# A fourth gate slab as seven block products in groups 2 to 8 of both feed-forward networks

## What is computed

```
x = x + 0.5 * _swiglu(_rmsnorm(x, ffn_norm), w_gu, w_down)

def _swiglu(h, w_gu, w_down):
    gate, up = jnp.split(h @ w_gu, 2, axis=-1)
    return (jax.nn.silu(gate) * up) @ w_down
```

## Time and profile before

| | us |
|---|---|
| median of 3 runs | 3013.56 |
| lowest, highest | 3011.37, 3015.36 |
| profiled execution, its own time | 3013.77 |
| its span in the trace | 3012.0 |
| TensorE busy | 2990.2 (99%) |
| VectorE busy | 2138.6 (71%) |
| GpSimd busy | 1531.6 (51%) |
| ScalarE busy | 1502.0 (50%) |

### The profile page before, as it was taken

The page is one execution under the profiler, slowest core; times in us unless marked ns, Lnnn a source line. Parts: engine busy times, 40 slices in busy tenths (PEclk is TensorE's granted clock), DMA queues, the critical chain, the costliest instruction groups (busy, mean ns, idle before and its releaser), DMA issues.

```text
span 3012.0 us, 48048 instructions
## 1 busy us (share of the span) xinstructions
PE 2990.2 (99%) x19120; PEld 2671.4 (89%) x19120; DVE 2138.6 (71%) x3446; ACT 1502.0 (50%) x1999; POOL 1531.6 (51%) x749
## 2 busy tenths in 40 slices
PE   8999999999999999999999999999999999999998
PEld 7888888888999999998888888888899998999997
DVE  4889886764324447787688887777579866789764
ACT  6555544444667455544555554444544454534454
POOL 5887764445565555585578876444550004710013
PEclk9999999999999999999999999999999999999999
DMA  6888887885776555566688888788576546666455
GB/s 217 288 278 271 278 280 247 305 288 181 229 176 176 158 165 148 151 171 201 200 284 282 266 281 287 242 306 277 173 216 194 162 147 216 181 190 182 154 182 181
DMA packets 491671, 663.43 MB, mean 220 GB/s; under 512 B 70440, under 2 KB 278040, under 8 KB 490936
## 3 DMA queue, kind: packets, MB, share of 16 engines
q1 hardware_dynamic: 485960, 655.85, 68.2%
q0 software_dynamic: 4448, 2.94, 0.4%
q10 hardware_dynamic: 1040, 1.58, 0.2%
HBM read 656.06 MB, written 2.11 MB: 219 GB/s over the span
## 4 chain that ended last, share of the span: by engine, by line
PE 95%; DVE 3%; ACT 1%; DMA 0%; issue 0%; POOL 0%; DVEq 0%; ACTq 0%
PE ps L1142 33%; PE ps L1006 20%; PE ps L1147 17%; PE ps L1012 10%; PE ps L1023 3%; PE ps L1175 2%; PE ps L1028 1%; PE ps L1171 1%; PE ps L990 1%; PE ps L1667 1%; DVE narrow_split_slabs L2261 1%; PE ps L1181 1%; PE ps L1443 1%; PE ps L1424 1%; PE ps L1178 1%; DVE h_split L2218 1%
## 5 line engine op out<-in xcount | busy, mean ns | idle before, releaser
L925 POOL TENSOR_TENSOR split_slabs<-stage,split_slabs 128x1024 fp32r<-128x1024 f32 x366 | 892.3, 2447 | 1005.4 <-ACT split_slabs L1723 999.4
L1723 ACT ACTIVATE split_slabs<-stage 128x1024 fp32r<-128x1024 f32 x544 | 573.4, 1059 | 558.3 <-PE ps L1147 435.8
L1723 ACT ACTIVATE narrow_split_slabs<-stage 128x1024 fp32r<-128x1024 f32 (+1 forms) x437 | 457.3, 1050 | 589.1 <-PE ps L1012 442.5
L1142 PE MATMUL ps<-split_slabs,h_split 128*128 128x512 f32 x2904 | 719.6, 390 | 0.8 <-ACT split_slabs L1723 0.8
L1142 PEld LDWEIGHTS ps<-split_slabs,h_split 128*128 128x128 f32 x2904 | 541.7, 188 | 111.4 <-ACT split_slabs L1723 1.2
L1006 PE MATMUL ps<-h_split,narrow_split_slabs 128*128 128x256 f32 x4928 | 620.6, 279 | 3.1 <-issue 1.9
L925 POOL TENSOR_TENSOR narrow_split_slabs<-stage,narrow_split_slabs 128x1024 fp32r<-128x1024 f32 (+1 forms) x182 | 441.2, 2434 | 315.8 <-ACT narrow_split_slabs L1723 315.5
L1006 PEld LDWEIGHTS ps<-h_split,narrow_split_slabs 128*128 128x128 f32 x4928 | 586.7, 188 | 13.0 <-issue 7.7
L2261 DVE TENSOR_TENSOR split_slabs<-stage,split_slabs 128x1024 fp32r<-128x1024 f32 x178 | 258.3, 1453 | 272.8 <-ACT split_slabs L1723 272.0
L2261 DVE TENSOR_TENSOR narrow_split_slabs<-stage,narrow_split_slabs 128x1024 fp32r<-128x1024 f32 x255 | 338.3, 1330 | 126.5 <-ACT narrow_split_slabs L1723 126.1
L1147 PE MATMUL ps<-split_slabs,h_split 128*128 128x512 f32 x1452 | 388.2, 389 | 0.0
(11 more groups left out here) (346 smaller groups left out, 3293.0 us busy)
## 6 DMA issues: line engine op xcount, KB each, us to landing
stage<-in_ffn_w_gu SPq DMA_DIRECT2D x352, 512.0 KB, 4.8
stage<-in_w_in SPq DMA_DIRECT2D x349, 512.0 KB, 3.7
U<-in_w_ada SPq DMA_DIRECT2D x192, 512.0 KB, 5.7
stage<-in_ffn_w_down SPq DMA_DIRECT2D x176, 512.0 KB, 5.2
stage<-in_w_out SPq DMA_DIRECT2D x96, 512.0 KB, 4.2
stage<-in_w_in SPq DMA_DIRECT2D x80, 128.0 KB, 2.9
stage<-in_w_branch_c SPq DMA_DIRECT2D x32, 192.0 KB, 3.4
stage<-in_cmp_w SPq DMA_DIRECT2D x8, 512.0 KB, 4.3
```

Of the source, the lines that this page charges most:

```text
L925: nc.gpsimd.tensor_tensor(slab_part(n, 1, size(n)), stage[:, n % RING, 0:size(n)], slab_part(n, 0, size(n)).bitcast(F32), ALU.subtract).th ...
L1142: mm(ps[:, 2 * pair + T, :], stationary(kk, i)[:, T * P:(T + 1) * P], w[0][:, kk, :], start=first and kk == 0 and i == 0, stop=False)
L1723: return fn(slab_part(n, 0, size(n)), stage[:, n % RING, 0:size(n)], ACT.Copy)
```

## The change

Gate slab 1 joins the summed slabs in groups 2 to 8 (not in group 1, where slab 3 remains the first), in both networks, so 14 slabs. As its sums are due before `gated` has freed the up side's banks, they stand in banks 4 and 5, into which the products of the same slab then go. Therefore ScalarE waits for `sum_gate` of the group before (`gate_summed`) ahead of the copy, and TensorE waits, ahead of the first product of slab 1, until VectorE has read the sums out (`slab_split`). Slab 3 now has the place of a second summed slab: its sums wait for `evacuated`, as they did. `combine`, `round_combined` and `rest_combined` use the length of `STR_SLABS` and so work on four slabs in place of three. `BY_VECTOR` is empty: the low part of slab 1 is GpSimd's (a plain slab in group 1; in groups 2 to 8 the plain blocks alone). The area for the combined parts grows, so the activations of group 7 may be written only after the gate of group 8 is done: ScalarE waits for that in `round_act`.

```diff
-STR_SLABS, STR_GROUPS = (3, 5, 7), range(1, 9)
+STR_SLABS, STR_GROUPS = (1, 3, 5, 7), range(1, 9)
+
+
+def first_summed(j):
+    return STR_SLABS[1] if j == STR_GROUPS[0] else STR_SLABS[0]
+
+
-BY_VECTOR = (1, 10)
+BY_VECTOR = ()
...
-HELD = 4 * STR_GROUPS[-1] * S
+HELD = 4 * (STR_GROUPS[-1] - 1) * S
...
-        summed = [s + 16 * j + q for s in (S_F1, S_F2) for j in STR_GROUPS for q in STR_SLABS]
+        summed = [s + 16 * j + q for s in (S_F1, S_F2) for j in STR_GROUPS for q in STR_SLABS if q >= first_summed(j)]
...
         def sums_of(n):
-            up = PAIR[G_F1 if n < S_MIX else G_F2]
-            return ps[:, 2 * up:2 * up + 2, :].rearrange("p b w -> p (b w)")
+            s0, up = (S_F1, PAIR[G_F1]) if n < S_MIX else (S_F2, PAIR[G_F2])
+            at = 4 if (n - s0) % 16 == STR_SLABS[0] else 2 * up
+            return ps[:, at:at + 2, :].rearrange("p b w -> p (b w)")
...
             if q == STR_SLABS[0]:
+                return gate_summed, len(STR_GROUPS) * (n >= S_MIX) + j - STR_GROUPS[0]
+            if q == STR_SLABS[1]:
                 return evacuated, g0 + j
...
                 pe.wait_ge(plain_hi, nth_sum[n])
+                if q == STR_SLABS[0]:
+                    pe.wait_ge(*slab_split(n))
...
-                                if (j, q) == (STR_GROUPS[0], STR_SLABS[0]):
+                                if (j, q) == (STR_GROUPS[0], first_summed(j)):
                                     pe.wait_ge(comb_ready, f + 1)
-                                summed_passes(gate_acc(f), n, q, q == STR_SLABS[0], q == 7)
+                                summed_passes(gate_acc(f), n, q, q == first_summed(j), q == 7)
...
             def round_act(f, j, k):
+                if (j, k) == (STR_GROUPS[-1] - 1, 0):
+                    act.wait_ge(slab_done, (S_F1, S_F2)[f] + 16 * STR_GROUPS[-1] + 8)
```

## The result

The changed kernel took 3022.57 us (median of 11 runs, 3021.07 to 3031.95), the kernel before beside it on the same chip 3014.9 us (11 runs, 3009.55 to 3020.35): ratio 1.0033 (it is not the quotient of the two medians), interval 1.0023 to 1.0042. It is slower, by 7.7 us by the medians and by some 10 us by the ratio (9.8 by the means), where 5.9 were forecast. Its profiled execution took 3025.76 us, of which the span is 3023.9, 11.9 more than the span before.

A forecast was written before the change was run, and what follows sets the result against it. TensorE was taken to bound the kernel, with 95% of the span. The terms -3.0 + 0.1 + 1.2 + 4.4 + 3.2 gave +5.9 us, so 3019.5 us against a median of 3013.56; range 3012.5 to 3025.

The forecast's parts named there:

- five terms: Matmuls -3.0 us, slab 1 of group 4 +0.1, of group 5 +1.2, group 0 of network 1 +4.4, of network 2 +3.2.
- Matmuls, -3.0: TensorE: 14 slabs become summed slabs, each 2.51 instead of 2.73 us, saving 3.0 us.
- Group 0, network 1, +4.4: Low passes of slab 13 wait 4.4 us: longer combined parts, and GpSimd's low part 14 goes between VectorE's operations.
- Rival A: Group 0: GpSimd does not pass VectorE, costs are 2.0 and 0.8 us, sum +1.1, 3014.7 us; chance 0.30.
- Group 0, network 2, +3.2: Low passes of slab 13: later combined low part and GpSimd going between cost 3.2 us; 0.8 without the passing.
- Slab 1 of group 5, +1.2: Network 1: VectorE reaches slab 1 late; TensorE stalls 2.9 us, less 1.7 for log_sigmoid meeting GpSimd's pause.
- Slab 1 of group 4, +0.1: Network 1: chain ends 0.9 us before TensorE needs it, VectorE's delay may use that; 0.1 us stall, between 0 and 0.9.
- Elsewhere at slab 1, 0: The other twelve summed slabs 1: the chain ends before TensorE needs it, cost 0.
- rival B: End of each group: VectorE cannot keep pace, TensorE waits at slab 1; +12.9 us, 3026.5 us; chance 0.16.
- GpSimd's added work, 0: 14 more operations of 1.9 us and two of 2.4 in group 1; GpSimd had 51% of the span; cost 0.
- Who goes first: Group 0: GpSimd, asking 0.36 us before the combined low part ends, goes ahead of VectorE's next queued operation, taking 2.4 us.

The follow-up runs named there:

- e2: The changed kernel with low part 14 made by VectorE instead of GpSimd in both groups 0; 3022.02 us, ratio 1.0031 to the kernel before.
- e8: The changed kernel with e3's order, slab 1 of group 5 of network 1 left as in the kernel before; 3015.73 us, ratio 0.9996 to the kernel before.
- e11: The changed kernel with e3's order, slab 1 of groups 4 and 5 of network 1 not summed; 3012.27 us, ratio 0.9997 to the kernel before.
- e12: The same kernel as e11, run once more; 3016.16 us, ratio 1.0010 to the kernel before.
- e9: The kernel before with BY_VECTOR empty, so GpSimd makes the low parts of slab 1 too; three slabs still summed; 3014.53 us, ratio 1.0002.
- e3: The changed kernel with combined parts rounded behind slab 14 and their low part made behind that of slab 13; 3017.58 us, ratio 1.0018 to the kernel before.
- e4: The changed kernel with log_sigmoid's five steps moved to group 1 of network 1, behind slabs 4 to 8; 3030.3 us, ratio 1.0059 to the kernel before.
- e6: The changed kernel with log_sigmoid's steps behind slab 0 instead of slab 14 of groups 2 to 6; 3025.27 us, ratio 1.0031 to the kernel before.
- e1: The changed kernel with slab 1 never summed; combined parts for four slabs and GpSimd's low parts stay; 3025.27 us, ratio 1.0038 to the kernel before.
- e7: The changed kernel with the moves of e3 and e6 together; 3017.63 us, ratio 1.0005 to the kernel before.

## Why the prediction was right, and where its sizes were off

The sign, the place of the largest cost and the size of three of five terms came out; the time was within the range and 3 us above the forecast. Part of that closeness is luck: the forecast of 3019.5 adds up from a median of 3013.56 for the kernel before, which is 3014.9 by all its runs, and the loss is 7.7 to 10 us, not 5.9. Of the +10.4 of the account, 4.5 are not in the sum: 2.6 of them at slab 1 of groups 4 and 5, 1.1 by the clock in slab 14, the rest in small sizes.

- **Matmuls, -3.0:** 14 x 0.18 = -2.5. The rows of one slab give 2.72 - 2.51 = 0.21; against before, the starts move by 0.18.
- **Group 0, network 1, +4.4:** +4.26, by the mechanism given, though the two agree better than they should: the low passes of slab 13 start 3.9 us later, since the combined parts came 0.4 us less late than reckoned, and the transposes at the half clock add 0.4. GpSimd's request came 0.35 us ahead of the end of the combined low part (0.36 was worked out) and passed VectorE, and e2 shows that it was this request. Rival A, in which it does not pass, fell. Not in the sum was the clock: +1.13 in slab 14, besides these 0.4.
- **Group 0, network 2, +3.2:** +3.57, in the same way.
- **Slab 1 of group 5, +1.2:** +2.8 with a wait of 2.64. **The step that failed** is the 1.7 us taken off because `log_sigmoid`, being later, would meet GpSimd's pause. GpSimd had been put off by just as much: its low part of slab 0 of group 5 went from 225.13 to 232.28 and the first step from 223.99 to 231.07, 7.1 us each, and so a step met that same operation again and took 2.36 us (2.27 before). The pause of the earlier trace rows had moved on with it, and began at 234.7. In the working only VectorE had been moved on. The upper bound, given as 2.9 (its own terms, 0.4 + 1.6 + 0.9 + 0.2, make 3.1), was the measured case.
- **Slab 1 of group 4, +0.1:** +1.1 with a wait of 0.93, just over the upper bound of 0.9. The step at 188.48 took 2.27 us (in the kernel before none there was over 0.2); the prediction has no such meeting at the end of group 3.
- **Elsewhere at slab 1, 0:** right in this execution: the other twelve show no wait. In e8, e11 and e12 one of them did. Of rival B the upper bounds of groups 4 and 5 came true, its 4.5 us in three more groups did not.
- **GpSimd's added work, 0:** the low parts by themselves cost nothing that e9 shows. What they do is widen the stretches in which a small instruction of VectorE's is caught (three steps at the end of group 4 in e9, one before). The operations on plain blocks were not tried by themselves.
- **Who goes first:** GpSimd, ready at 51.91, went ahead of VectorE's next instruction, which was queued directly behind one that ended at 52.26 (49.97 + 2.29). The Trainium skill (SBUF — State Buffer, Who interferes with whom) says that the order of issue decides who blocks, and the rows agree with that.

In short: the change costs VectorE 1.1 to 1.2 us a group, net, by its idle time ahead of `gated` in groups 2 and 3, where it had 1.6 or less to spare, and puts a longer chain into group 0. Of the 10.4 us, some 9 hang on the place of the combined parts (4.26 + 1.13 + 3.57, gone in e3). The 3.9 at slab 1 of groups 4 and 5 go with the steps of `log_sigmoid` that meet GpSimd, on top of VectorE's delay; how much is due to either no run separates, as both moves of the steps (e4, e6) brought waits of their own.

**Open.** Why the clock fell behind some waits and not behind others (below). Why the loads of slab 0 came later in some executions. Whether `log_sigmoid` on another engine, or in the down stage, would leave a gain; that was not tried. The differences of the unchanged parts were not followed up, nor the 4.5 us by which the ratio of e3 exceeds its own steps.

## What to carry to other kernels

When a change puts off one engine, move every engine whose instructions hold it up to its new time as well before counting on a pause seen in the old trace; the bound without the pause is the safer figure. The spare time of the engine that gets the work is read at its own waits for the bottleneck (here `gated`'s idle time, 1.63, 1.07 and 0.38 us in groups 2 to 4 of the kernel before): work beyond that is handed on from group to group. A long instruction that the bottleneck does not need yet (the combined parts) belongs behind those that it waits for.

## What the runs showed of the hardware

- **The clock.** In the changed kernel the granted clock fell to 0.50, the 1.2 GHz level, for some 3.4 us behind waits of 1.97 and 2.58 us that lay close together, and stayed at 1.00 behind the wait of 2.64 us in group 5 and behind the 0.40 and 2.58 us of network 2. Behind this last pair it did fall in e1, e4 and e6. Behind single waits it fell at 2.05 us (e3), 2.47 (e1), 2.80 (e2) and 5.78 (e4), where eight high passes took 3.78 us instead of 1.98, and it stayed at 2.20 (e7) and 2.61 (e2). So the length of the wait alone does not tell; what does stays open. In the changed kernel and in e3 the fall cost 1.5 (1.13 and 0.40) and 1.35 us on top of the wait.
- **Small instructions.** On 32 elements VectorE took 0.18 us, and 2.12 to 2.42 when it began within the first 0.33 us of a GpSimd instruction of 2.4 us; begun later in one, it took less. Each of the 49 steps of over 0.6 us in network 1, in all traces, ended 0.04 to 0.05 us behind the end of the GpSimd instruction that it met. This held both for tensor_tensor with two inputs in SBUF and for tensor_scalar with one. With GpSimd's instructions back to back, three steps in a row (e1) or every second one (e9) were caught.
- **A difference of 0.65 us** in when GpSimd starts went with one of 1.65 us in TensorE's wait (e3 and e8), and one kernel gave both cases in two executions (e11 and e12): own steps of -0.9 and +3.3 us. One profile is one draw of that.
